# A fused diffusion-transformer layer: two token halves from attention through the FFN, and the output prefill moved into the FFN

## The reference, cut to what matters

```python
# per batch; D = 1024, 8 query heads, 2 kv heads, head 64, window +-128, FFN hidden 2816
mod_x = split(silu(c) @ w_ada + b_ada, 6)              # shift, scale, gate, twice
hc = modulate(layer_norm(ctx), mod_c[0], mod_c[1])     # 256 context tokens
kc, vc = context_kv(hc, w_in)
h = modulate(layer_norm(x), mod_x[0], mod_x[1])
q, k, v, u, vb, ga, gb = split(h @ w_in)
ya = window_attention(rope(q), rope(k), v, kc, vc, sink)
yb = gelu(u) * (w_s @ layer_norm(gelu(vb)) + b_s)      # per 128-token chunk
merged = sigmoid(ga) * (ya @ w_a) + sigmoid(gb) * (yb @ w_b)
x_mid = layer_norm(2**0.25 * x + mod_x[2] * (merged @ w_o)) * ln1_g + ln1_b
h2 = modulate(layer_norm(x_mid), mod_x[3], mod_x[4])
ffn = (silu(h2 @ w_gate) * (h2 @ w_up)) @ w_down
out = layer_norm(2**0.25 * x_mid + mod_x[5] * ffn) * ln2_g + ln2_b
```

## Time and profile before

| what | value |
|---|---|
| time, median of three runs | 1136.14 us |
| time of the profiled execution | 1132.06 us |
| its span (slowest core, 6) | 1130.5 us |
| spans of the eight cores | 1120.6 to 1130.5 us |
| TensorE (PE) busy | 902.6 us, 80% |
| VectorE (DVE) / ScalarE (ACT) / GpSimd (POOL) busy | 572.4 / 326.0 / 365.5 us |
| moved by DMA | 106.87 MB |

### The profile page before, as it was taken

How to read it: one execution, slowest core, us unless ns; L and a number is a source line. 1 busy time by engine, 2 the same in 40 slices (tenths; PEclk the granted TensorE clock), 3 DMA queues, 4 the chain that set the end, 5 groups by cost and what they waited for, 6 DMA issues and landing times.

```text
span 1130.5 us, 15140 instructions; the slowest of 8 cores (1120.6 to 1130.5 us)
## 1 busy us (share of the span) xinstructions
PE 902.6 (80%) x5272; PEld 435.6 (39%) x5357; DVE 572.4 (51%) x995; ACT 326.0 (29%) x493; POOL 365.5 (32%) x333
## 2 busy tenths in 40 slices
PE   1100699987877898999878499999999999999960
PEld 1100345544434443444334244444444444444420
DVE  2002385445756655222368426565555656566780
ACT  0100366456545524322235621111111111111321
POOL 6000476430424335232447540111011011010775
PEclk9999999998988999999989789999999999999995
DMA  8999930157878766330667550330231132100466
GB/s 220 175 163 208 186 94 20 20 77 109 144 140 148 134 153 121 57 54 8 123 166 172 131 131 1 75 75 4 71 75 21 54 75 38 38 1 1 75 111 113
DMA packets 38442, 106.87 MB, mean 95 GB/s; under 512 B 3808, under 2 KB 4960, under 8 KB 37856
## 3 DMA queue, kind: packets, MB, share of 16 engines
q0 software_dynamic: 25760, 57.61, 32.0%
q1 hardware_dynamic: 12608, 48.29, 15.0%
HBM read 129.94 MB, written 16.78 MB: 130 GB/s over the span
## 4 chain that ended last, share of the span: by engine, by line
PE 69%; issue 7%; DMA 7%; ACT 5%; DVE 5%; another core or an unknown queue 5%; POOL 2%; DVEq 0%; POOLq 0%; ACTq 0%
PE psum L993 26%; PE psum L1010 13%; PE psum L864 9%; PE psum L873 4%; DMA arena<-wada 4%; PE psum L932 3%; PE psum L666 3%; PE psum L715 2%; PE psum L704 2%; DMA arena<-arena 2%; PE psum L823 2%; ACT arena L794 2%; ACT arena L957 1%; DVE arena L520 1%
## 5 line engine op out<-in xcount | busy, mean ns | idle before, releaser
L993 PE MATMUL psum<-arena 128*128 128x512 bf16 x1380 | 318.9, 382 | 6.0 <-ACT arena L957 4.5
L993 PEld LDWEIGHTS psum<-arena 128*128 128x128 bf16 x1408 | 138.7, 99 | 172.9 <-issue 10.2
L1020 DVE TENSOR_TENSOR arena<-psum,arena 128x1024 f32<-128x1024 f32 x144 | 170.2, 1219 | 13.3 <-PE psum L1010 7.3
L1010 PE MATMUL psum<-arena 128*128 128x512 bf16 x689 | 165.6, 381 | 6.1 <-DVE arena L523 2.1
L997 ACT ACTIVATE arena<-psum 128x512 f32<-128x512 f32 x88 | 52.5, 596 | 363.2 <-PE psum L993 358.6
L998 DVE TENSOR_TENSOR arena<-psum,arena 128x512 bf16<-128x512 f32 x88 | 60.9, 691 | 168.6 <-PE psum L993 161.1
L864 PE MATMUL psum<-arena 128*128 128x512 bf16 x495 | 120.4, 392 | 13.7 <-DVE arena L551 6.2
L520 DVE BATCH_NORM_STATS2 arena<-arena 128x6 f32<-128x512 f32 x152 | 97.4, 682 | 32.1 <-DMA arena<-xh 13.8
L525 POOL TENSOR_TENSOR arena<-arena 128x1 f32<-128x1 f32 x84 | 51.2, 641 | 166.1 <-DVE arena L524 163.4
L1010 PEld LDWEIGHTS psum<-arena 128*128 128x128 bf16 x704 | 68.7, 98 | 90.3 <-issue 10.0
L876 DVE SCALAR_TENSOR_TENSOR arena<-arena,psum 128x512 f32<-128x512 f32 x64 | 43.9, 687 | 104.9 <-PE psum L873 80.6
(11 more groups left out here) (93 smaller groups left out, 966.5 us busy)
## 6 DMA issues: line engine op xcount, KB each, us to landing
arena<-xh SPq DMA_DIRECT2D x34, 512.0 KB, 6.2
arena<-wada POOLq DMA_DIRECT2D x24, 512.0 KB, 11.4
arena<-wc POOLq DMA_DIRECT2D x16, 768.0 KB, 10.0
arena<-wff POOLq DMA_DIRECT2D x11, 1024.0 KB, 10.4
arena<-wff SPq DMA_DIRECT2D x22, 512.0 KB, 5.9
out<-ln2b SPq DMA_DIRECT2D x16, 512.0 KB, 54.3
arena<-arena POOLq DMA_DIRECT2D x16, 512.0 KB, 6.2
out<-arena POOLq DMA_DIRECT2D x16, 512.0 KB, 5.7
```

Of the source, the lines that this page charges most:

```text
L993: i = e.matmul(bk(b0 + x), lhsT=w[:, k, 256 * x + fi * 128:256 * x + (fi + 1) * 128], rhs=h2T[:, k, tok], start=(k == 0), stop=(k == 7))
L1010: x = e.matmul(bk(b0 + half), lhsT=actb[r % 2][:, fi, t * 128:(t + 1) * 128], rhs=w2[r % NWR][:, fi, half * 512:(half + 1) * 512], start=( ...
L1020: G.op('dve', lambda e: e.tensor_tensor(out=acc, in0=bk(b0, 2), in1=acc, op=ALU.add))
```

## The change

- **Two halves.** A2 still makes u and vb of all groups, but q, k and v only for groups 0 and 1 (tiles 0 to 9); those of groups 2 and 3 are written between attention of tiles 0 to 7 and of tiles 8 to 15. The merge of groups 0 and 1 is written after attention, then c2 of tiles 0 to 7, then the merge of groups 2 and 3, then c2 of tiles 8 to 15.
- **The FFN too.** Tiles 0 to 7 go through all 11 rounds, then tiles 8 to 15, so each FFN weight is loaded and scaled twice (22 rounds of 1024 tokens). The first half's tail runs while the second half computes.
- **Down products** accumulate over two rounds in PSUM (three in the last set of a half) before DVE adds them.
- **Held back.** The 16 output copies wait for a late operation of the second set of the FFN. Loads of x beyond the first four tiles, the rotary tables and the small tables wait for the last of the eight first `w_ada` blocks (`wl`).
- Eight of the later `w_ada` blocks move into A2. Down weights are staged in quarters (256 KB) through two 2 KB-per-partition buffers, not in halves. Accumulations are written in pieces of four matmuls (`mm`), which lets the planner put other work between them. Exp waits for the last Gelu. Buffers are laid out anew, banks of PSUM are handed out anew.

```diff
-    def op(self, eng, fn, dur=None, prio=None):
+    def op(self, eng, fn, dur=None, prio=None, after=()):
...
+        for p in after:
+            deps[p.id] = True
...
+    B67 = Banks(6, 7)
+    k_unit(2, B67)
...
-    for j in range(4):
+    for j in range(8):
         att(j)
-        ada_step()
+        ada_step(bk_misc())
+    for g in (2, 3):
+        if g == 3:
+            k_unit(3, B67)
+            k_unit(4, B67)
+        for m in range(4):
+            q_unit(m, g, B67)
+            v_unit(2 * g + 6 + m if g == 2 else 14 + m, B67)
+    for i in range(3):
+        c1_load(i)
+    for j in range(8, NT):
+        att(j)
+        wout_step(j - 8)
+    for m in range(8):
+        for g in range(2):
+            c1_unit(m, g, B67)
+        c1_load(m + 3)
...
-    for t in range(NT):
-        G.op('sp', lambda e, t=t: e.dma_start(out=out_d[t * 128:(t + 1) * 128, :], in_=ln2b_d))
...
+        sets = [(0, 1), (2, 3), (4, 5), (6, 7), (8, 9, 10)]
+        seq.append((half, [tuple(base + r for r in s) for s in sets]))
+    GUB = Banks(0, 1, 6)
...
+        for q in range(8):
+            t = 8 * half + q
+            dn(s, t, 2 if n < 2 or dn_i[0] % 2 == 0 else 4)
+            dn_i[0] += 1
+            if lastset:
+                tail(t)
...
+            for u in fill[lo:hi]:
+                u()
...
+        if n == 1:
+            o = G.ops[-1]
+            load(ln2g, ln2g_d)
             for t in range(NT):
-                dn([r], t)
...
+                G.op('sp', lambda e, t=t: e.dma_start(out=out_d[t * 128:(t + 1) * 128, :], in_=ln2b_d), after=[o])
```

More of the change, by code:

```diff
@@ L510, in build_nc, with mm, f, stats @@
+    def mm(out, pairs, part=4):
+        n = len(pairs)
+        for i0 in range(0, n, part):
+            def f(e, i0=i0):
+                for i in range(i0, min(i0 + part, n)):
+                    r = e.matmul(out, lhsT=pairs[i][0], rhs=pairs[i][1], start=(i == 0), stop=(i == n - 1))
+                return r
+            o = G.op('pe', f)
+        return o
     st_i = [0]
-    def slot():
+    def stats(src, n):
         s = st_i[0] % NST
         st_i[0] += 1
-        return stt[:, s], mvr[:, s]
@@ L561, in bc_block @@
         load(bslice, badabc_d[:, gi * 256:(gi + 1) * 256])
[L563 to L567, removed]
+        mm(pb, [(scb[:, k, :], w[:, k, :]) for k in range(8)])
         dst = (g2bc if which else g1bc)[:, q * 256:(q + 1) * 256]
+        G.op('dve', lambda e: e.tensor_tensor(out=dst, in0=pb, in1=bslice, op=ALU.add))
         if which == 0:
-            G.op('dve', lambda e: e.tensor_tensor(out=dst, in0=pb, in1=bslice, op=ALU.add))
@@ L688, in v_unit @@
         dst = (vaug if kind == 'x' else vcaug)[:, ti, :, 0:64]
[L689 to L700 removed]
+        pv = bk(banks())[:, 0:128]
@@ new lines, in vn, with vb_unit @@
+    def vn(t):
+        return vnp[t // 8][:, t % 8]
+    def vb_unit(t, banks):
+        pq = bk(banks())
+        mm(pq, [(hT[:, k, (t + 1) * 128:(t + 2) * 128], wvb[:, k, :]) for k in range(8)])
+        gv = gvb[t % 3]
+        gelus.append(G.op('act', lambda e: e.activation(out=gv, in_=pq, func=AF.Gelu_apprx_tanh)))
+        rstd, nmr = stats(gv, 512)
+        G.op('pool', lambda e: e.tensor_scalar(out=vn(t), in0=gv, scalar1=rstd, scalar2=nmr, op0=ALU.mult, op1=ALU.add))
+    att_i = [0]
+    bk_qk = Banks(0, 2)
@@ new lines, in ab, with gu @@
+    def ab(i):
+        return actb[i % 3] if i < 6 else actb[i % 6]
+    gu_i = [0]
+    def gu(i, tg, fi, banks):
+        sg = sgb[gu_i[0] % 2]
+        gu_i[0] += 1
+        w = w1[i % 3]
+        tok = slice((tg % 2) * 512, (tg % 2 + 1) * 512)
+        ps = []
+        for x in range(2):
+            ps.append(bk(banks()))
+            mm(ps[x], [(w[:, k, 256 * x + fi * 128:256 * x + (fi + 1) * 128], h2T[:, k, tg * 512:(tg + 1) * 512])
+                       for k in range(8)])
+        G.op('act', lambda e: e.activation(out=sg, in_=ps[0], func=AF.Silu))
+        G.op('dve', lambda e: e.tensor_tensor(out=ab(i)[:, fi, tok], in0=ps[1], in1=sg, op=ALU.mult))
@@ new lines, in dn @@
+    def dn(rounds, t, b0):
+        tk = slice((t % 8) * 128, (t % 8 + 1) * 128)
+        for half in range(2):
+            mm(bk(b0 + half), [(ab(i)[:, fi, tk], w2[i % 5][:, fi, half * 512:(half + 1) * 512])
+                               for i in rounds for fi in range(FG)])
+        acc = xmid[t]
+        if rounds[0] % NR == 0:
+            G.op('dve', lambda e: e.scalar_tensor_tensor(out=acc, in0=acc, scalar=ALPHA, in1=bk(b0, 2), op0=ALU.mult,
+                                                         op1=ALU.add))
+        else:
+            G.op('dve', lambda e: e.tensor_tensor(out=acc, in0=bk(b0, 2), in1=acc, op=ALU.add))
@@ L734, in build_nc @@
         for m in range(4):
-            q_unit(m, g)
-            u_unit(m, g)
+            u_unit(m, g, A2B)
+            if g:
+                if m < 3 and ada_i[0] < 8:
+                    ada_step(A2B())
         for t in range(4 * g, 4 * g + 4):
-            v_unit(t)
-            vb_unit(t)
-    k_unit(4)
-    pq = bk(bank2())[:, 0:CTX]
-    def f(e):
-        for k in range(8):
-            i = e.matmul(pq, lhsT=wqk[:, k, 512:640], rhs=hcT[:, k, :], start=(k == 0), stop=(k == 7))
-        return i
```

849 lines of the change are left out of this document (381 added, 468 removed).

## The result

The changed kernel takes 0.9262 of the time of the kernel before, 95% interval 0.9227 to 0.9298: of 1135.93 us some 84 go, which leaves 1052. (Four executions gave 1051.73, 1053.45, 1077.64 and 1081.74 us; in the last two one die was disturbed, whence a median of 1065.55 that is above what the undisturbed ones show.) The profiled execution took 1051.73 us with a span of 1049.8 (core 6; the eight cores 1039.6 to 1049.8). The forecast was 1039 us, 1004 to 1080; against that same execution its sum was 1035.2.

What follows compares the result with a forecast made beforehand. PE bounds the FFN, DMA the lead-in. PE's busy 902.6 - 6 plus idle 52 + 14 + 32 + 10 + 29 gave 1033.6 us of span, 1035.2 of time; adjusted to the median, 1039, range 1004 to 1080.

Steps and rivals of the forecast that it cites:

- Lead-in: Before the first projection: 52 us of PE idle, w_ada landing near 41, first k unit near 60; never below 45.
- Projections: Projections before attention: 14 us of PE idle, 6 for starving and 8 for the old waits; ends 5 and 30.
- I take 6 for that starving: Projections: 6 us of PE idle while remaining weights and ten tiles of x still arrive.
- the forecast's own mark for a wrong step: First projection to FFN: over 60 us of PE idle there would show a step wrong.
- some 100: Stages up to the FFN: some 100 us less idle time, as a sign that the forecast is right.
- Attention and merge: Attention through first post-norm: 32 us idle where 58.8 stood, filled by moved q, k, v and merge; ends 15 and 59.
- FFN with the copies: FFN and its seam with post-norm: 10 us of PE idle, 44 us of copies just covered; ends 2 and 45.
- second rival: FFN: down weights queued behind 44 us of copies lose their cover, adding 35 us, to 1074; chance 0.10.
- Down adds "at nothing": FFN: adds fall from 160 to 80, saving DVE 97.5 us; costed at nothing because matmuls hide it.
- Staging in quarters at nothing: FFN down weights: a quarter takes at most 7.4 us, 14.8 a round of 20.7 with two buffers, so hidden.
- fourth rival: FFN down weights: staging buffers fail to overlap, adding 196 us, to 1235; decides from 5.2 us a quarter; chance 0.04.
- Last set and tail: End of kernel: 29 us of PE idle where 37.9 stood, at 4.3 us a tail; ends 24 and 40.

Runs made afterwards that it cites:

- run with late loads: Changed kernel with rotary columns from 1152 on and later w_ada blocks waiting for a Gelu, context tiles moved to the projections' third group: 1044.98 us, ratio 0.9216.
- spread copies: Changed kernel with the 16 output copies issued one after each step of the FFN's second and third set, not in one block: 1044.55 us, ratio 0.9206.
- combined kernel: Changed kernel with late loads, spread copies, third x pair ungated, power first on POOL, a buffer per late tile, every second late multiply on DVE: 1019.9 us, ratio 0.8978.

## Why the prediction was right or wrong

The forecast of a gain was right and its range held the time; the profiled execution came 16 us above the sum. The largest cause, the copies, is shown: they are worth 47 or 48 of the 84 us. What the other 34 to 36 come from is shown only in part. Term by term:

- **Lead-in: 52 forecast, 42.5 measured,** below the 45 under which nothing was to let it fall. `w_ada` ended at 39.66 us (41 forecast). The first projection came at 50.56, not 60, for x and the rotary piece, which the sum put behind wqk, moved beside it. That the copies held the queues is shown twice, by putting them back (+47) and by moving them alone in the kernel before (-48).
- **Projections: 14 forecast, 33.4 measured. This is the step that failed,** in "I take 6 for that starving"; and its upper end of 30 was reached. The bytes were counted, but not their order: rotary columns for later groups stood on SP's queue ahead of tiles of x, and two later `w_ada` blocks and the context moved while PE waited for x. A late tile also stops work that is ready, by DVE's order. The run with late loads gave back 5 to 8 us of it. With those loads and the third pair of x rearranged, the stretch holds 118.7 - 104.84 = 13.9 us idle (of the 33.4, some 3 are matmuls without a record). So the forecast's own mark for a wrong step, over 60 us idle from first projection to FFN, was passed (33.4 + 36.1 = 69.5), by the projections, not by the middle. The stages up to the FFN hold 66 us less idle time; the sum's terms made it 80, and the text's "some 100" did not even agree with them.
- **Attention and merge: 32 forecast, 36.1 measured,** with the clock at 0.99; busy time over the whole span is 893.6, 3.0 under the forecast. Near in size, but by luck, for the reason is not borne out. The moved q, k and v are worth nothing, since the merge takes their room where they are gone. Of the 83 us of merge only about a quarter ran beside attention; holding the merge back costs 29 us, but the kernel before had more of the merge there and idled more. So filler was not what was new. The accumulations in pieces account for 4 to 6 us. What else makes attention shorter (157.9 us in the kernel before with late copies, 137.8 here), and the stretch behind it, whose idle time fell from 26.5 to 13.8, no run takes apart: other banks, the product with V in two halves, eight `w_ada` blocks fewer beside attention, the new order of merge and c2.
- **FFN with the copies: 10 forecast, 11.4 measured,** 6.40 of it the one late down weight behind the copies. The second rival's mechanism was there, but small; the spread copies remove it.
- **Down adds "at nothing": nearly.** In the FFN the 96 further adds, 117 us of VectorE, cost under 4 us; but with one round in the last set some 8 are lost there, which the forecast had not seen. The kernel before has two rounds in its last set, the changed one three; what that step alone is worth no run shows.
- **Staging in quarters at nothing: right.** The fourth rival, from 5.2 us a quarter on, did not come: with 0.3 for the issue, 4.9 for the landing and 1.3 for the scaling a quarter takes 6.5 us, with two buffers in turn 3.3, and PE waited for a weight once, behind the copies. The Trainium skill, "DMA: Bandwidth & Descriptors", section Bandwidth, wants DMAs of at least 1 MiB for three quarters of peak. That did not decide here: the DMA share in the FFN is 0.64.
- **Last set and tail: 29 forecast, 32.9 measured.** The 4.3 us a tail counted POOL's work, not its order: DVE waited 6.13 and 9.07 us for a power of under 1 us queued behind multiplies. Eight buffers alone changed nothing. In the combined kernel the tail is 18.2 us; which share is the power's place, which the multiplies moved to DVE, and which the buffers with these two, was not tried apart.

Summed: -9.5 in the lead-in, +19.4 in the projections, +4.1 in the middle, +1.4 in the FFN, +3.9 at the end, -3.0 of busy time make 16.3, the 16.2 by which the span of 1049.8 stands above 1033.6.

## What to carry to other kernels

Ahead of the first dense stage, write down the order in which bytes are needed and hold back whatever comes later, large prefills first of all; a count of bytes gives the start of the stage, and the order decides whether it starves. Where PE waits in a chain over several engines, look for independent matmuls that can lie beside it, and then count what really ran there: a quarter of this merge cost attention no time and kept the granted clock at 0.99 in place of 0.88, while q, k and v lengthened it by 11 us and won nothing in the end. Where one short operation sits on a busy engine that works in order, in the middle of a chain, look at its place before adding buffers: buffers alone won nothing here, and with the power first and half the multiplies moved the tail fell from 32.4 to 18.2 us.

## What the runs showed of the hardware that was not expected

- Sixteen copies of 512 KB issued together landed in 35.6 us (median), let go one per step in 6.4. Loads of 256 KB on the same queue landed in 4.9 us, and in 4.8 to 6.3 in the other runs with this staging; 512 KB took 5.9, and 5.6 with the copies held back. Half the size landed no sooner to speak of, with other traffic beside it (DMA share in the FFN 0.64 and 0.22).
- In two executions of nearly the same program, the changed kernel and that with eight buffers, the stretch from 50.6 to 100.5 us had a granted clock of 0.69 and 0.90 on the profiled core, with 22.47 and 23.50 us busy and spans within 1.2 us. Where PE waits for loads, the lower level of 1.2 GHz cost nothing that the end shows.
